# The last two pieces of each output matrix in the order of token halves: the first half's two accumulator banks ahead

## The reference, cut to what matters

```python
def rms_norm(x, g):
    y = x32 * lax.rsqrt(jnp.mean(x32 * x32, axis=-1, keepdims=True) + RMS_EPS)
def gated_post_add(x, y, g_post, gate, weight):          # first block
    return x + weight * gate[:, None, :] * rms_norm(y, g_post)
def swiglu_ffn(h, w_in, w_out):
    g, u = jnp.split(h @ w_in, 2, axis=-1)               # 1024 -> 2 x 2816
    return (jax.nn.silu(g) * u) @ w_out                  # 2816 -> 1024
h = h + HALF * _swiglu(_rmsnorm(h, g), w_in, w_out)      # second block
h = h + u @ w_out                                        # second block, mixer
```

## Time and profile before

| | |
|---|---|
| median of three runs | 2405.29 us (2403.14 to 2405.49) |
| the profiled execution | 2402.39 us, its span 2400.6 us |
| TensorE busy | 2311.4 us, 96% of the span |
| VectorE busy | 1752.7 us, 73% |
| ScalarE busy | 1275.5 us, 53% |
| TensorE share of the chain that ended last | 77% (VectorE 10%, ScalarE 6%) |
| mean granted clock | 0.995 |

### The profile page before, as it was taken

How to read it: one execution, slowest core, us unless ns; L and a number is a source line. 1 busy time by engine, 2 the same in 40 slices (tenths; PEclk the granted TensorE clock), 3 DMA queues, 4 the chain that set the end, 5 groups by cost and what they waited for, 6 DMA issues and landing times.

```text
span 2400.6 us, 44999 instructions
## 1 busy us (share of the span) xinstructions
PE 2311.4 (96%) x16696; PEld 2049.0 (85%) x16696; DVE 1752.7 (73%) x2779; ACT 1275.5 (53%) x1942; POOL 27.5 (1%) x66
## 2 busy tenths in 40 slices
PE   7999999999999999999999999999999999999998
PEld 7888978888888768888889898888888888888887
DVE  6888988888988677767667575766666676747666
ACT  5445454454445565446446562654554475536444
POOL 0000000000000000000000000000000000000000
PEclk9999999999999999999999999999999999999999
DMA  9886978868997316655555441455555543415553
GB/s 328 276 294 235 357 262 293 289 222 285 327 316 263 106 54 209 225 199 165 189 188 176 131 148 37 161 190 187 189 177 187 191 165 127 147 33 170 195 192 123
DMA packets 130438, 480.67 MB, mean 200 GB/s; under 512 B 14608, under 2 KB 14784, under 8 KB 129776
## 3 DMA queue, kind: packets, MB, share of 16 engines
q1 hardware_dynamic: 128448, 467.62, 57.7%
q0 software_dynamic: 1840, 10.93, 1.2%
HBM read 477.41 MB, written 1.07 MB: 199 GB/s over the span
## 4 chain that ended last, share of the span: by engine, by line
PE 77%; DVE 10%; ACT 6%; issue 4%; DMA 2%; SPq 0%; DVEq 0%; ACTq 0%; POOLq 0%; POOL 0%
PE bank L601 75%; ACT work L1413 2%; DMA ring<-weights 2%; DVE w_lo L2071 2%; ACT w_hi L1413 2%; DVE y L2105 2%; PE bank L630 1%; ACT h_split L1413 1%; ACT L1413 1%; DVE y L2261 1%; PE bank L1227 0%; DVE work L2502 0%; DVE y L2634 0%; ACT y L1413 0%; DVE x L2266 0%
## 5 line engine op out<-in xcount | busy, mean ns | idle before, releaser
L601 PE MATMUL bank<-h_split,w_hi 128*128 128x256 f32 (+1 forms) x5344 | 1152.4, 336 | 26.8 <-ACT work L1413 9.3
L2071 DVE TENSOR_TENSOR w_lo<-ring,w_hi 128x1024 fp32r<-128x1024 f32 x715 | 871.2, 1222 | 353.4 <-ACT w_hi L1413 352.3
L1413 ACT ACTIVATE w_hi<-ring 128x1024 fp32r<-128x1024 f32 x726 | 765.8, 1057 | 625.9 <-PE bank L601 533.2
L601 PEld LDWEIGHTS bank<-h_split,w_hi 128*128 128x128 f32 x5344 | 901.5, 191 | 121.3 <-issue 13.8
L601 PE MATMUL bank<-h_split,w_lo 128*128 128x256 f32 x3896 | 754.1, 283 | 0.1
L601 PEld LDWEIGHTS bank<-h_split,w_lo 128*128 128x128 f32 x3896 | 613.6, 191 | 24.4 <-DVE w_lo L2071 0.5
L1413 ACT ACTIVATE work<-bank 128x512 f32<-128x512 f32 (+1 forms) x266 | 154.8, 586 | 327.1 <-PE bank L601 298.5
L601 PE MATMUL bank<-w_hi,act_hi 128*128 128x512 f32 x704 | 275.4, 391 | 0.2
L601 PE MATMUL bank<-w_lo,act_hi 128*128 128x512 f32 x704 | 274.9, 390 | 0.0
L601 PE MATMUL bank<-w_hi,act_lo 128*128 128x512 f32 x704 | 273.9, 389 | 0.0
L2105 DVE CUSTOM_DVE_ANT_0 y<-ring,v_first 128x1024 f32<-128x1024 f32 x160 | 189.4, 1220 | 1.7 <-DMA ring<-weights 1.7
(11 more groups left out here) (226 smaller groups left out, 1569.7 us busy)
## 6 DMA issues: line engine op xcount, KB each, us to landing
ring<-weights SPq DMA_DIRECT2D x886, 512.0 KB, 4.9
work<-cmp POOLq DMA_DIRECT2D x1, 4096.0 KB, 15.1
sq<-rows POOLq DMA_DIRECT2D x6, 512.0 KB, 7.6
work<-lora POOLq DMA_DIRECT2D x2, 1024.0 KB, 5.9
x<-x_in SPq DMA_DIRECT2D x1, 1024.0 KB, 5.7
out<-y SPq DMA_DIRECT2D x2, 512.0 KB, 2.6
const_sb<-consts POOLq DMA_DIRECT2D x1, 726.0 KB, 8.3
v_first<-c_in SPq DMA_DIRECT2D x1, 512.0 KB, 3.6
```

Of the source, the lines that this page charges most:

```text
L601: return nc.tensor.matmul(out, lhsT, rhs, start=start, stop=stop, skip_group_check=skip)
L1413: return nc.scalar.activation(out, in_, f, bias=bias, scale=scale, **kw)
L2071: tt(w_lo[q % SLOTS][:, :], ring[n % RING][:, c * HALF:(c + 1) * HALF], w_hi[q % SLOTS][:, :].bitcast(F32), ALU.subtract).then_inc(halves_ ...
```

## The change

The last two pieces are no longer multiplied one after the other. The order is now: the last but one piece into banks 0, 1, 2; the last piece into banks 0 and 1; the last but one piece into bank 3; the last piece into banks 2 and 3. The multiplications are the same, 24 in all. The slot of the last but one piece is released after its bank 3. TensorE checks the waits of a piece each time it turns to it, four times in place of two. The same is done in `out_linear`.

```diff
-            def spread(w, a_hi, a_lo, start, stop):
+            def spread(w, a_hi, a_lo, start, stop, to=range(4)):
-                for b in range(4):
+                for b in to:
                     t, c = slice(b // 2 * P, (b // 2 + 1) * P), slice(b % 2 * 512, (b % 2 + 1) * 512)
                     ins = mm3(bank[b][:, :], a_hi[:, t], a_lo[:, t], w_hi[w][:, c], w_lo[w][:, c], start, stop)
                     if stop and b < 3:
                         ins.then_inc(y_sums, 1)
                 return ins
...
+            LAST_TWO = ((0, (0, 1, 2)), (1, (0, 1)), (0, (3,)), (1, (2, 3)))
+            def last_downs(st, q):
+                for i, to in LAST_TWO:
+                    hh = HALVES - 2 + i
+                    half_wait(q + i)
+                    pe.wait_ge(hidden_ready, HALVES * st.ffn + hh + 1)
+                    a = slice(hh % 2 * TOK, (hh % 2 + 1) * TOK)
+                    ins = spread((q + i) % SLOTS, act_hi[:, a], act_lo[:, a], False, i == 1, to)
+                    if 3 in to:
+                        ins.then_inc(half_used, 1)
...
-                down(st, q + 6 * FFN_STEPS - 2, HALVES - 2)
-                down(st, q + 6 * FFN_STEPS - 1, HALVES - 1)
+                last_downs(st, q + 6 * FFN_STEPS - 2)
...
-                for k in range(KC):
+                for k, to in [(k, range(4)) for k in range(KC - 2)] + [(KC - 2 + i, to) for i, to in LAST_TWO]:
                     q = st.half + k
                     half_wait(q)
                     pe.wait_ge(h_ready, 8 * st.pre + k + 1)
-                    spread(q % SLOTS, hi3[:, k, :], lo3[:, k, :], k == 0, k == KC - 1).then_inc(half_used, 1)
+                    ins = spread(q % SLOTS, hi3[:, k, :], lo3[:, k, :], k == 0, k == KC - 1, to)
+                    if 3 in to:
+                        ins.then_inc(half_used, 1)
```

## The result

The changed kernel takes 2412.89 us (median of eight runs, 2408.97 to 2415.76), the kernel before 2405.24 in the same comparison: a ratio of 1.0032, interval 1.0023 to 1.0042. That is 7.65 us more, between 5.5 and 10.1. The forecast was 2413.6, 8.3 more.

What follows compares the result with a forecast made beforehand. The prediction took TensorE as the limit, with 77% of the chain of waits. 7.9 us of delay at nine places plus 0.4 for weight loads made 8.3, so 2405.29 became 2413.6 us, range 2409 to 2418.

Steps and rivals of the forecast that it cites:

- The head start gives 0.: Banks 0 and 1 end 0.68 us earlier, VectorE's four banks end unmoved: 0; rival, it counts: 2399.2 us, chance 0.04.
- The slot's release holds the squares.: Piece 20's slot is released 1.36 us later; ScalarE's next high part waits, squares queue behind it: 7.9 us in all.
- for 1.06, so the first square at 510.18: First block, ScalarE: high part from 509.11 takes 1.06 us, so the first square starts 1.01 us late.
- how they run already, so nothing of it is regained: First block: squares already follow each other at 0.61 us, so the delay stays, 0.96 us a place.
- The places without loss: At 767 us TensorE's other work covers the delay; after the last network no high part follows: 0 at both.
- The two norms beside GpSimd's memset: Norms before a long mixer, 1276 and 1926 us: delay partly covered, 0.5 to 0.95 us each, taken as 0.6.
- a cover of 0.43: At those two norms VectorE sets the second reciprocal, so the root's delay has 0.43 us of cover.
- The weight loads: Last piece begins a step earlier, its weight load may not run ahead: 0.05 us at eight networks, 0.4 in all.
- the cover of 0.17: Last piece's first multiplication at 506.81, hidden activations ready at 506.64: 0.17 us of cover where there was 0.86.
- The waits: TensorE's two more waits for every piece turned to, 22 turns more: 0, at most 22 x 0.05 us.
- The clock: Rival: TensorE's longer gap before the first block's transposes lowers the clock, 1.6 us a fall; two give 2416.8; chance 0.12.
- the nine places: Delayed stretches: four first-block at 0.96 us, three second-block at 0.94, two norms at 0.6; 7.9 in all.

Runs made afterwards that it cites:

- experiment 3: Changed kernel with the high part of the next matrix's second piece left out at ten places, a one-column copy instead: 2406.12 us (1.0004).
- experiment 1: Kernel before, old bank order; only ScalarE's high part of the next matrix's second piece held until the last piece's bank 1 is whole: 2410.83 us (1.0023).
- experiment 2: Kernel before with the high part of the next matrix's second piece left out at ten places, a one-column copy instead: 2406.21 us (1.0003).
- 4: Changed kernel with bank 3 of the last but one piece one step earlier, so only bank 0 of the last piece precedes it: 2407.11 us (1.0008).
- 5: Changed kernel with ScalarE making the held high part after the second square (first block: also after the first root), not before the first: 2407.23 us (1.0006).
- experiment 6: Changed kernel with banks 2 and 3 of the last but one piece both after banks 0 and 1 of the last: 2419.40 us (1.0059).
- experiment 7: Changed kernel's code with the old order of banks, in four turns with their waits: 2405.09 us (0.9999).
- experiment 8: Changed kernel with three more unread multiplications (21, not 18) behind each output product of the first block: 2413.72 us (1.0030).

## Why the prediction was right

**The head start gives 0.** Right, and shown twice: in the changed kernel the bank operations end 1.13 us after the last multiplication begins against 1.12, and in experiment 3 it has a free way and all places stay. The reason is in the two paces: VectorE needs 0.67 to 0.69 us a bank and TensorE 0.68 us a step, so that VectorE is done about one bank's time after bank 3 is whole, however early the first two were.

**The slot's release holds the squares.** Right as a mechanism: experiment 1 has the loss without the order, experiment 3 beside its base, experiment 2, the order without the loss, 4 half the delay with hardly any loss, 5 the same late release with nothing critical queued behind it. The sizes were too large. Forecast 0.96, 0.94 and 0.6 a place, measured 0.67, 0.83 and 0.53; 7.9 in all against 6.2. Two terms of it:

- "for 1.06, so the first square at 510.18": the next activation starts 0.96 after the high part does, not 1.06 (511.02 to 511.98; 1558.08 to 1559.05 gives 0.97). That is 0.10 at every place. The Trainium skill has it ("ScalarE: Activation LUTs", What ACT_TABLE_LOAD costs: activations back to back overlap by about 93 ns), and the traces agree; I added durations where starts were to be counted.
- "how they run already, so nothing of it is regained": in the first block something is. The second root of the product waits for GpSimd's addition, and that took 0.67 us beside VectorE's update of x (from 511.45) and takes 0.48 now (from 514.21):

```profile
511.30 1.42 DVE L2266 SCALAR_TENSOR_TENSOR x<-y,small,x 128x512 f32<-128x512 f32 x2
511.45 0.67 POOL L2013 TENSOR_SCALAR small<-small 128x1 f32<-128x1 f32 x1 [1.29 <-ACT sq L1413]
```

```profile
513.87 1.42 DVE L2280 SCALAR_TENSOR_TENSOR x<-y,small,x 128x512 f32<-128x512 f32 x2
514.21 0.48 POOL L2027 TENSOR_SCALAR small<-small 128x1 f32<-128x1 f32 x1 [1.26 <-ACT sq L1427]
```

From the fourth square to the root it is 0.94 us before (511.27 to 512.21, with 0.26 of idle time) and 0.75 after (514.03 to 514.78). That is 0.19, and 0.05 came back between the squares: the first square is 0.91 late and the root 0.67. Why GpSimd is faster there can be read from the traces. VectorE's update began 0.15 us before GpSimd's addition (511.30) and now begins 0.34 before it (513.87), and both times the addition ends 0.82 us after the update's start. It does so at all ten additions beside an update in the trace before and at all ten in the one after, whether they start 0.15 or 0.35 behind it, and 0.07 us after the update's first instruction has ended; alone an addition takes 0.20 or 0.21. So GpSimd's addition waits there for VectorE's instruction, and an update that begins earlier lets it go earlier. The Trainium skill, "GPSIMD Engine Reference", 1. Specifications, has GpSimd share its interfaces to the on-chip memory with VectorE, with contention where VectorE's instruction reads two inputs from it, as the update of x does; the traces agree.

**The places without loss.** Right: 767 has +0.01 and the last stage none.

**The two norms beside GpSimd's memset.** Taken at 0.6, they have 0.52 and 0.53, but not by the way that the prediction took. It let the second half's root, less a cover of 0.43, set the loss; with the 0.83 by which that root is late this would give 0.40. The loss came by the first half. Before, at 1276 us (product end 1277.80), and then after (product end 1283.71):

```profile
1278.90 0.28 ACT L1413 ACTIVATE small<-small 128x1 f32<-128x1 f32 x1
1279.44 0.15 DVE L2196 RECIPROCAL small<-small 128x1 f32<-128x1 f32 x1
```

```profile
1285.64 0.28 ACT L1427 ACTIVATE small<-small 128x1 f32<-128x1 f32 x1
1285.95 0.16 DVE L2210 RECIPROCAL small<-small 128x1 f32<-128x1 f32 x1 [0.52 <-ACT small L1427]
1286.15 0.95 DVE L2215 TENSOR_SCALAR work<-x,small 128x512 f32<-128x512 f32 x1
1287.02 0.14 DVE L2210 RECIPROCAL small<-small 128x1 f32<-128x1 f32 x1
```

The first root is 0.83 late (1.10 us after the last multiplication begins, now 1.93). Its reciprocal had 0.23 of cover (1279.44 less 0.31 less 1278.90) and comes 0.60 late; VectorE has idled 0.52 us for the root. The scaling behind it still meets the memset, in 0.95 us in place of 1.03, and the second reciprocal follows it without idle time, 0.53 late. That the size came near is luck here.

**The weight loads.** Forecast 0.05, measured 0.09 at each network of the second block, within the bounds. The load stands 0.06 us ahead of its multiplication (508.60 and 508.66), where the load for the same step had 0.22 before (506.59 and 506.81). Before, then after:

```profile
506.59 0.19 PEld L601 LDWEIGHTS bank<-w_hi,act_hi 128*128 128x128 f32 x1
```

```profile
508.21 0.19 PEld L601 LDWEIGHTS bank<-w_hi,act_lo 128*128 128x128 f32 x1
508.60 0.19 PEld L601 LDWEIGHTS bank<-w_hi,act_hi 128*128 128x128 f32 x1 [0.20 <-issue]
```

It starts 0.12 after the hidden activations are ready (508.06 + 0.42 = 508.48), so of the cover of 0.17 nothing is left, and experiment 6, one step further, pays 0.68 more: 0.77. The rule that the prediction quoted from the Trainium skill ("TensorE: Matmul & The Clock Gate", Part 2), that TensorE pulls the next weight load ahead of the running multiplication, agrees with the trace: the load lost its lead first. The size that the prediction set beside it, 0.1 a network, was nearer than the 0.05 that it took.

**The waits** cost nothing (experiment 7).

**The clock.** The rival was not the cause, and not absent either. The clock fell at two of the four places with the longer gap in the changed kernel's trace, at 5 of 12 over the three traces that have it, and a fall cost 0.1 us where TensorE waits for others behind it and 1.3 to 1.4 at 1085, close to the 1.6 of the forecast. The prediction's sign of it, a mean granted clock under 0.995 by more than a few thousandths, was set by one execution of the kernel before; its runs have 0.9932 in the mean of 57. What rules the clock out as the cause is that experiment 8, with the gap filled and no fall at any of these places, has the same loss at each of them, as 508 and 1085 have in the changed kernel.

So 6.2 + 0.7 = 6.9 us are accounted for by stretches, of 7.65 measured with an interval from 5.5 to 10.1; falls of the clock may be part of what is left, which these runs can't show. The sign, the nine places and the held high part were right. The places' sizes were up to 0.29 us too large, 1.7 in all; the weight loads were 0.3 too small, and the falls, put at nothing, worked the same way. That 8.3 lies so near 7.65 owes something to luck.

## What to carry to other kernels

Before a producer's order is changed to finish one part earlier, compare the consumer's time per part with the producer's: where they are equal, the last part sets the end and an early start is lost as idle time in the middle. And look at what else the moved instruction releases: here it was a buffer, whose refill stood in ScalarE's queue ahead of the critical work. Time such a change by the short stretch around it: 0.02 us there against 2 us in the total.

## What the runs showed of the hardware

At the four places of the first block, where some 4 us of small multiplications stand before the gap, the clock fell behind 5 of 12 gaps of 1.84 to 1.92 us, and behind none of 28 gaps of 1.23 to 1.25. A fall that met TensorE waiting for others cost about 0.1 us (316), one at 1085 cost 1.3 to 1.4, and in dense work it is about 1.6 by the earlier trace rows. A weight load that waits for its data starts 0.11 to 0.12 us after the data's producer ends, and its multiplication 0.04 to 0.06 later; the stream then loses 0.09 us although the data had 0.17 us of cover on paper. GpSimd's small addition takes 0.20 us alone; beside VectorE's update of x it ends 0.82 us after that update begins, whenever it began itself.
